# Down projections of an fp32 transformer pair: both parts of an activation tile in one 512-column matmul

## The reference

```python
def _conv_ffn(x, w_up, conv_w, conv_b, w_down):
    u = _causal_dwconv(x @ w_up, conv_w, conv_b)
    gate, up = jnp.split(u, 2, axis=-1)
    return (jax.nn.silu(gate) * up) @ w_down          # [256, 2816] @ [2816, 1024]

def swiglu(h, w_gate, w_up, w_down):
    return (jax.nn.silu(h @ w_gate) * (h @ w_up)) @ w_down

# first block:   x = x + _moba(...);  x = x + _conv_ffn(...)
# second block:  x = x + 0.5 * (1 + ga1) * swiglu(...)
#                x = x + (1 + ga2) * hybrid_mixer(...)
#                x = x + 0.5 * (1 + ga3) * swiglu(...)
```

## Time and profile before

| | |
|---|---|
| median of 3 runs | 850.05 us |
| the profiled execution | 847.64 us, its span 845.4 us |
| TensorE busy | 808.8 us (96%) |
| weight loads busy | 787.5 us (93%) |
| VectorE busy | 644.1 us (76%) |
| ScalarE busy | 489.7 us (58%) |
| mean granted TensorE clock | 0.994 |

### The profile page before, as it was taken

How to read it: one execution, slowest core, us unless ns; L and a number is a source line. 1 busy time by engine, 2 the same in 40 slices (tenths; PEclk the granted TensorE clock), 3 DMA queues, 4 the chain that set the end, 5 groups by cost and what they waited for, 6 DMA issues and landing times. The chain is left out here.

```text
span 845.4 us, 16845 instructions
## 1 busy us (share of the span) xinstructions
PE 808.8 (96%) x6824; PEld 787.5 (93%) x6824; DVE 644.1 (76%) x1331; ACT 489.7 (58%) x1015; POOL 21.0 (2%) x53
## 2 busy tenths in 40 slices
PE   6799998999999999999999999799989999999998
PEld 5798887999999999999999999778878999999998
DVE  5678767998998887999888787867646797665651
ACT  6745545766666655756555556656645675555540
POOL 1000000000000000000000000700000000000000
PEclk9999999999999999999999999999999999999999
DMA  9757463766665997499988886445214678765540
GB/s 297 268 193 233 139 224 125 250 199 200 215 198 175 307 307 267 125 304 337 344 293 287 291 268 214 128 127 186 88 60 144 198 233 290 225 200 181 190 154 26
DMA packets 151069, 179.44 MB, mean 212 GB/s; under 512 B 5712, under 2 KB 141136, under 8 KB 150992
## 3 DMA queue, kind: packets, MB, share of 16 engines
q1 hardware_dynamic: 149536, 177.65, 64.1%
q10 hardware_dynamic: 432, 0.68, 0.2%
q0 software_dynamic: 1024, 0.03, 0.1%
HBM read 177.27 MB, written 1.05 MB: 211 GB/s over the span
## 5 line engine op out<-in xcount | busy, mean ns | idle before, releaser
L914 DVE TENSOR_TENSOR wlo<-raw,whi 128x512 fp32r<-128x512 f32 x528 | 342.7, 683 | 69.1 <-ACT whi L671 68.5
L1291 PE MATMUL bank<-A,whi 128*128 128x256 f32 x1280 | 367.6, 287 | 13.3 <-DVE wlo L914 8.3
L671 ACT ACTIVATE whi<-raw 128x512 fp32r<-128x512 f32 x528 | 308.6, 621 | 107.4 <-PE bank L1293 97.4
L1292 PE MATMUL bank<-A,whi 128*128 128x256 f32 x1280 | 359.8, 281 | 0.0
L1293 PE MATMUL bank<-A,wlo 128*128 128x256 f32 x1280 | 359.7, 281 | 0.0
L1291 PEld LDWEIGHTS bank<-A,whi 128*128 128x128 f32 x1280 | 246.0, 192 | 16.8 <-DVE wlo L914 8.5
L1292 PEld LDWEIGHTS bank<-A,whi 128*128 128x128 f32 x1280 | 244.1, 191 | 1.0 <-issue 1.0
L1293 PEld LDWEIGHTS bank<-A,wlo 128*128 128x128 f32 x1280 | 243.7, 190 | 0.0
L1291 PE MATMUL bank<-Hhi,whi 128*128 128x256 f32 x528 | 146.0, 277 | 0.0
L1293 PE MATMUL bank<-Hhi,wlo 128*128 128x256 f32 x528 | 145.8, 276 | 0.0
L1292 PE MATMUL bank<-Hlo,whi 128*128 128x256 f32 x528 | 145.8, 276 | 0.0
(11 more groups left out here) (148 smaller groups left out, 783.2 us busy)
## 6 DMA issues: line engine op xcount, KB each, us to landing
mring<-in_w_mod SPq DMA_DIRECT2D x72, 512.0 KB, 6.2
raw<-in_ffn_w_up SPq DMA_DIRECT2D x22, 1024.0 KB, 5.1
raw<-in_w_gate SPq DMA_DIRECT2D x22, 1024.0 KB, 5.9
raw<-in_w_up SPq DMA_DIRECT2D x22, 1024.0 KB, 5.9
raw<-in_w_down SPq DMA_DIRECT2D x16, 1024.0 KB, 5.4
raw<-in_w_in SPq DMA_DIRECT2D x12, 1024.0 KB, 5.8
raw<-in_moba_w_qkv SPq DMA_DIRECT2D x11, 1024.0 KB, 6.3
raw<-in_ffn_w_down SPq DMA_DIRECT2D x8, 1024.0 KB, 6.4
```

Of the source, the lines that this page charges most:

```text
L671: act.activation(whi[:, i % SPL, k0:k1, 0:width], raw[:, i % RAW, k0:k1, 0:width], ACT.Copy).then_inc(s_whi, 1)
L914: dve.tensor_tensor(lo, raw[:, i % RAW, k0:k1, 0:width], hi.bitcast(F32), ALU.subtract).then_inc(s_wlo, 1)
L1291: pe.matmul(o, hi, xh, start=kg == 0 and not (j and halved(g)), stop=False)
L1292: pe.matmul(o, hi, xl, start=False, stop=False)
```

## The change

In the three down phases the hi and lo parts of a hidden tile lie side by side in one tile `H` of 512 columns. One matmul moves them both through the hi weights into all 512 columns of the bank: hi x hi into the left half, hi x lo into the right half. The third matmul (lo weights, hi activations, 256 columns) adds to the left half. The two halves are added as the bank is emptied: the eviction adds (or gates and adds) the left half to `XT`, then the right half, with a wait between the two because both write the same tile. The other phases are as they were.

```diff
@@ build_program: tiles
-            Hhi = scope.enter_context(nc.sbuf_tensor("Hhi", [P, KF, S], F32R))
-            Hlo = scope.enter_context(nc.sbuf_tensor("Hlo", [P, KF, S], F32R))
+            H = scope.enter_context(nc.sbuf_tensor("H", [P, KF, 2, S], F32R))
+        Hhi, Hlo = H[:, :, 0, :], H[:, :, 1, :]
@@ semaphores and tables
-        s_xeven, s_xscaled = sem("s_xeven"), sem("s_xscaled")
+        s_xhalf, s_xeven, s_xscaled = sem("s_xhalf"), sem("s_xeven"), sem("s_xscaled")
+        down_g = {g: k + 1 for k, g in enumerate(g for g, x in enumerate(groups) if x[1] == "down")}
@@ vector engine
+            def add_gated(gate, n, b, done=None):
+                x = XT[:, n, :]
+                if not gate:
+                    ins = dve.tensor_tensor(x, b, x, ALU.add)
+                else:
+                    ins = dve.scalar_tensor_tensor(out=x, in0=b, scalar=hcol[:, n:n + 1], in1=x, op0=ALU.mult, op1=ALU.add)
+                return ins.then_inc(done, 1) if done else ins
@@ evict, tags "o" and "down"
-                        x, b = XT[:, n, :], at(g, i)
+                        b = at(g, i)
...
-                        if not gate:
-                            ins = dve.tensor_tensor(x, b, x, ALU.add)
-                        else:
-                            ins = dve.scalar_tensor_tensor(out=x, in0=b, scalar=hcol[:, n:n + 1], in1=x,
-                                                           op0=ALU.mult, op1=ALU.add)
+                        if tag == "down":
+                            add_gated(gate, n, b, s_xhalf)
+                            need.wait_ge(s_xhalf, 2 * down_g[g] - 1 + i)
+                            b = at(g, i, S, 2 * S)
+                        ins = add_gated(gate, n, b)
@@ multiply
-                for j in range(1 if tag == "f" else 2):
+                for j in range(2 if tag == "down" else 0):
+
+                    b = banks[2 * (g % 2) + j]
+                    hi, lo = whi[:, i % SPL, kt, j * P:j * P + P], wlo[:, i % SPL, kt, j * P:j * P + P]
+                    pe.matmul(b[:, :], hi, H[:, kg, :, :].rearrange("p a b -> p (a b)"), start=kg == 0, stop=False)
+                    ins = pe.matmul(b[:, 0:S], lo, xh, start=False, stop=last and kt == nk - 1)
+                for j in range(0 if tag == "down" else 1 if tag == "f" else 2):
```

## The result

Four runs of the changed kernel took 855.39 to 856.72 us, median 855.87, against 850.51 us (four runs, 848.76 to 852.48) before: a ratio of 1.0063, 95% interval 1.0039 to 1.0088. The forecast was 848.0 us, range 844.5 to 852.0, so the time is 3.9 us above the range and on the other side of no change. The profiled execution took 856.11 us with a span of 853.9, 8.5 us more than the span before.

A forecast was written before the change was run, and what follows sets the result against it. TensorE's own pace, set by weight loads, was taken to bound the down phases. Steps -3.8, end evictions +1.04, qkv3 start +0.8 and up2 start 0 gave -2.0 us, from 850.05 to 848.0 us, range 844.5 to 852.0.

The forecast's parts named there:

- What the 113 ns consist of: Down phases: each 256-column matmul's 113 ns was said to be the time of one 128-column weight load.
- The size of the long matmul: Down-phase step: 512 fp32r columns take 213.3 ns with the load hidden; with the short matmul, 333 ns instead of 340.
- -3.8 us: Down phases: gain from 7.3 ns saved on each of 528 steps.
- gained up to 6.4 us: Down phases: best case, with a step of 328 ns.
- The upper bound: Down phases: slowest step of 342.6 ns, each matmul keeping 11.3 ns over its columns; 1.2 us lost.
- Rival 3: Down phases: the slow pace takes hold, step 342.6 ns, 853.1 us; chance 0.10.
- The evictions: Second adds on DVE: +1.04 us at the kernel's end, +0.8 at the start of qkv3, 0 at up2.
- Carrying the sum from one profile to the median: Whole kernel: -2.0 us on the profile's 847.64 was applied to the median 850.05, giving 848.0 us.
- Rival 1: Down phases: step of 328 ns, the short matmul keeping the 113 ns pace; 845.5 us, chance 0.20.
- Rival 2: Down phases: only a fixed instruction cost of about 2 ns per removed matmul falls away; 850.8 us, chance 0.08.
- Rival 4: Down phases: 512 fp32r columns run at the plain fp32 rate, step 541 ns, +106 us; chance 0.02.
- Rival 5: Down1: DMA or DVE becomes the bound, the 2.6 us gain of down1 and down2 goes; 850.6 us, chance 0.08.

The follow-up runs named there:

- experiment 1: Kernel of its own with TensorE alone running rows of one matmul kind: 227 ns for 512 fp32r columns, 120 for 256, 353 for the alternating pair.
- experiment 3: Kernel before the change with Hhi and Hlo moved by 64 bytes, nothing else: 857.84 us, ratio 1.0071 to the kernel before.
- experiment 4: Changed kernel with tile H moved by 64 bytes in its partition, nothing else: 852.76 us, ratio 1.0020 to the kernel before.

## Why the prediction was wrong, by its steps

- **What bounds the down phases** was right: TensorE's pace, with DVE, ACT and the loads behind it. The profile shows no wait of TensorE inside a down phase, also with DVE 2.6 us busier in down1.
- **What the 113 ns consist of** was the step that failed. I read the 0.11 to 0.12 us between two loads around one-column matmuls as the cause of the 113 ns of the earlier trace rows, because the numbers agreed. It is not what the pace waits for: a load of half the columns left 117 ns where the full one had 120, and moving the activation tile by 64 bytes changed 113 to 120 with the same loads (experiments 1 and 3).
- **The size of the long matmul.** From that came 213.3 ns for 512 fp32r columns, taken from plain fp32 records of the same length. Those have only 2.4 ns beyond two cycles a column (429.1 ns for 512 columns in experiment 1); fp32r has 226.7 for 512 at best, 13.4 ns beyond one cycle a column, and had 235.5 here. The term "-3.8 us" was mis-sized and had the wrong sign: it measured +7.0 in the profile (13.3 ns x 528). With 0.4427 ns as the least that any fp32r column cost, the step could not have come under 340 ns, so "gained up to 6.4 us" was never there.
- **The upper bound** of the step, 342.6 ns, spread the slow pace's extra as a fixed cost on each matmul. Here it was 22 ns on 512, and TensorE alone had from 13.4 to 20. Rival 3 named the right pace (that of the 22.7 us stretch of the earlier trace rows) and the right point from which it decides, with 853.1 us for 10%; scaled by columns it gives 2 x 118 + 118 = 354 ns, +7 + 1.8 on the profile's 847.64, that is 856.4 us, and 856.11 were measured. The range stopped below it, because the extra of a 512-column matmul was taken as no larger than that of one with 256.
- **The evictions**: 1.92 us against 1.92 forecast for L1147, 1.67 against 1.68 for L1145, 0.74 against 0.8 at the start of qkv3, 0.86 against 1.04 at the end, nothing at the start of up2; together 1.6 us against 1.8.
- **Carrying the sum from one profile to the median** failed as well. All down phases of the profiled execution had the fast pace, and others of the same kernel have the slow one. The prediction did say that the pace behind a one-column matmul depends on what ran ahead, but only for up2 and up4; the down phases are behind such a matmul too. That this execution was 2.4 us under the median could have warned me, and I took the difference as the same before and after. It was not: against the profile the change is +8.5 us, against the median +5.4.
- **Rivals 1, 2, 4 and 5** did not occur: 354 ns was a step, not 328, 338 or 541, and DMA moved 275 GB/s with no wait of TensorE for it.

## What to carry to other kernels

Before a matmul is widened to save weight loads, find out whether the load is what its pace waits for; an equal duration elsewhere does not show it, a row of the same type with a shorter load or another place would. Where a kernel's pace has more than one lasting value, take two profiles before a sum is made, and give a change of sequence the slower pace as its first rival. A stride or a pad that was right for one width need not be right for another: compare two widths at more than one place before the width is judged.

## What the runs showed of the hardware that was not expected

- An fp32r column cost between 0.4427 and 0.469 ns at the upper clock level (2.4 GHz), depending on where the moving tile lies in its partition and on the sequence of widths: 113.3 to 120.0 ns for 256, 226.7 to 233.3 for 512 alone, 346.7 to 353.3 for the pair. bf16 had 109 and 216, plain fp32 429 for 512.
- 64 bytes of shift are worth 6.6 ns on each 256-column matmul of the down phases: 63.3 against 59.8 us from the first to the last start of a phase. The place of the weights counts too: 120.0 against 117.8 ns with TensorE alone.
- The same instructions at the same place hold either of two paces for a whole phase of 60 us, 113.3 or 117.8 ns once settled. In the full kernel a one-column matmul between two streams of 256 columns reversed the pace at 127 of 127 places; with TensorE alone, at offsets 0 and 48, it did not change it (120.0 and 113.3 ns). Why it does the one here and the other there, and what sets the pace at the start of a phase, was not settled.
- The pair of 512 and 256 columns had two paces as well, 346.7 and 353.3 ns. In experiment 4 the two fast phases came behind streams at 117.8 ns and the slow one behind 113.3; three phases are too few to call that a rule.
- That the reads of the moving tile and of the weights get in each other's way is a reading that fits the dependence on either one's place, and no run shows it directly.
